# Peer experts of the first half: dots before sums, sums shared two to one between TensorE and VectorE, projected tiles copied by ScalarE, keys loaded earlier

## The chip, the core and the metric

The kernel runs on one core of a Trainium2 chip. The metric is the device time of one execution in microseconds (us). PE is TensorE, DVE is VectorE, ACT is ScalarE, POOL is GpSimd, SP is SyncE.

## What is computed

Two blocks of a network over 512 tokens of width 1024, all in float32. The change touches the first block, above all its layer of "peer" experts:

```python
q = (xb @ w_query).reshape(T, 8, 2, 128)                  # 8 heads, two halves of a query
s = einsum('thpk,hpnk->thpn', q, sub_keys)                # scores against 128 keys
top_s, top_i = top_k(s, 16)                               # 16 best of each, 256 pairs, 16 best pairs
best_s, best_pos = top_k(cand_s, 16); idx = ...; gate = softmax(best_s)
u = expert_u[idx]; v = expert_v[idx]                      # a row of 1024 floats for each pick
act = gelu(einsum('td,thkd->thk', xb, u))                 # "dots"
y = einsum('thk,thkd->td', gate * act, v)                 # "sums"
```

Each token has 8 x 16 = 128 picks. For each pick and each tile of 128 tokens one row of the table u and one of the table v are gathered (128 partitions x 4 KB, 524,288 bytes). Ahead of the peer layer stands a mixer (a projection to 3584 columns, a gated linear recurrence named hgrn, a short convolution, an output projection), behind it the second block.

## The kernel before

The tokens are split into half A (tiles 0 and 1) and half B (tiles 2 and 3). Half A runs first through the first mixer, its query projection and the picks of tile 0. Then a long block opens (`Stretch`) in which half B's mixer, query projection and picks run as the main work, and the peer layer of half A runs beside them on DVE, POOL and PE. Stages inside it end with `meet`, where SP, PE, ACT and DVE wait for each other; POOL does not take part.

**The side work.** `Peer.sequence` writes a fixed plan of steps: one step is one gathered row, either a dot (table u) or a sum (table v). POOL gathers the rows in the order of the plan into a ring of 12 slots (L1496); slot n is refilled once step n-12 has been consumed. A dot is one fused multiply-and-accumulate on DVE (L1574). A sum of tile 1 is one fused multiply-add on DVE (L1580), and each waits for the one before. A sum of tile 0 goes by PE: DVE makes a diagonal matrix of the coefficients (L1568, eight buffers), and PE multiplies the gathered row with it, adding up in banks 0 and 1 (L1593, four matmul records for a row). A sum needs the Gelu of its tile's dots, which ACT does at the first `meet` after the tile's last dot has been put in the program (L1508).

In the plan before, the 128 dots of tile 0 come first, then 98 dots of tile 1 (`FRONT` = 226), then 32 groups of four PE sums of tile 0 and one further dot of tile 1 (30 dots are left), then the 128 DVE sums of tile 1.

**Who places the steps.** The code of the main work calls `beside(m, dve, us)` at many places. `Peer.go` adds that time to a credit and places steps while the credit is at least `pace`: in the front a dot costs 1.1 of credit, later a DVE step costs 1.8 and a PE sum 0.75. PE sums are allowed from `reach_front` on, which `key_scores` calls once half B's scores of its first tile are copied; `reach_front` first places what is missing up to `FRONT`. What the credit did not place by the end of half B's picks is placed in `Peer.finish`, a stage of its own with nothing else in it but a prefetch of 4 MB of weights, which waits for the last PE sum.

**Half B's stages, in order**, with their names in the prediction:
- first projection: 12 tiles of 128 columns (L345 on PE, 16 matmul records for a tile; `project`). DVE copies each tile out of its bank (L1046). In `setup`, ahead of the first copy, DVE finishes the picks of tile 0 (`pick_rest`): its last part waits for an exponential on ACT (L1313, issued by `exp_next`, which is passed as `other`). Between the tiles DVE does the 14 parts of tile 1's picks.
- second projection: 16 tiles, copied by DVE (L1049), with the short convolution in `setup`
- hgrn in three stages, and a group norm
- output projection: 8 tiles, kept by a multiply-add on DVE (`add_projected`, L1060)
- norm; SP issues the loads of the keys into `keys_raw` (L1112)
- turn back: PE transposes h into rows (L1085) and then the keys (L1125), ACT copies the latter (L1132)
- query projection: 16 tiles, copied by DVE (L1706)
- scores and picks (`key_scores`): PE multiplies queries and keys (L1232), DVE copies tile 0's scores (L1249), ACT tile 1's (L1240); DVE picks, 14 parts for each of two tiles, with 5.0 us of credit behind each part
- finish: the rest of the plan; then PE's sums are copied out of the banks (L1603)

After that the norms and the second block's mixer of half A follow, with half B's peer steps beside them.

## Time and profile before

| | us |
|---|---|
| median of 3 runs | 3729.78 (3722.16 to 3733.29) |
| profiled execution, its own time | 3702.43 |
| span of its profile | 3700.6 |

Over the whole span the page gives PE 74% busy, DVE 58%, POOL 35%, ACT 16%, and 272 GB/s moved by DMA; 40 equal slices of the span show DVE at 7 to 9 tenths from the fifth slice to the twenty-third. The change touches the stretch from 372 to 1298 us of the span. A timeline row reads: start, duration, engine, line, operation, output <- input, count, and in brackets the idle time before it with what ended it. Durations of DVE overlap slightly: the start-to-start time of two neighbours is what an instruction costs its engine.

### The profile page before, as it was taken

What the parts mean: (1) busy time and instruction counts of PE and PEld (TensorE: products, weight loads), DVE (VectorE), ACT (ScalarE), POOL (GpSimd) and SP (SyncE); (2) the same over time, 40 slices, a digit from 0 to 9 for tenths busy, and PEclk for the clock granted to TensorE, in tenths of its full rate; (3) what the DMA queues carried; (4) which work ended last, traced back from release to release, by engine and by line L of the source; (5) the groups of instructions that cost most, each with busy time, mean ns of one, the idle gap of its engine ahead of it and who ended that gap; (6) DMA issues with size and microseconds to landing.
All of it is one profiled execution on the core that took longest, in us unless ns stands there. A gap on an engine that the chain in (4) does not pass through costs nothing. (4 is left out here: it accounts for less than half of the span.)

```text
span 3700.6 us, 44636 instructions
## 1 busy us (share of the span) xinstructions
PE 2746.5 (74%) x17746; PEld 1979.5 (53%) x17746; DVE 2136.4 (58%) x3975; ACT 592.3 (16%) x1229; POOL 1311.7 (35%) x1082
## 2 busy tenths in 40 slices
PE   5977553678880086889885757799999789777777
PEld 4866443464330075677773636478888667322232
DVE  6544999878748977968777988424222453200001
ACT  1021002200000012122212310132222330100001
POOL 0001366666767765757655566300000000000000
PEclk7988776788995587889987778999999889899998
DMA  7616588888999988889979699622333324899997
GB/s 273 229 40 222 198 293 317 299 326 328 329 343 370 376 310 302 312 309 369 356 259 362 219 336 363 227 91 87 101 101 96 117 80 172 331 428 428 428 429 321
DMA packets 390749, 1006.30 MB, mean 272 GB/s; under 512 B 30381, under 2 KB 234515, under 8 KB 375699
## 3 DMA queue, kind: packets, MB, share of 16 engines
q0 software_dynamic: 150912, 549.52, 40.0%
q1 hardware_dynamic: 211856, 406.65, 29.9%
q10 hardware_dynamic: 27779, 47.38, 3.5%
q8 instruction: 134, 2.20, 0.2%
q14 instruction: 68, 0.56, 0.0%
HBM read 971.99 MB, written 31.46 MB: 271 GB/s over the span
## 5 line engine op out<-in xcount | busy, mean ns | idle before, releaser
L1496 POOL DMA_INDIRECT ring<-in_peer_u_dram,index x512 | 685.0, 1338 | 448.0 <-DVE ring L1574 240.4
L1496 POOL DMA_INDIRECT ring<-in_peer_v_dram,index x512 | 597.4, 1167 | 334.6 <-DVE h_rows_b L1580 144.6
L345 PE MATMUL bank<-hT,weights 128*128 128x256 f32 x1984 | 459.3, 396 | 144.5 <-ACTq L142 72.3
L345 PEld LDWEIGHTS bank<-hT,weights 128*128 128x128 f32 x1984 | 394.6, 200 | 208.6 <-issue 130.0
L1891 PE MATMUL bank<-hT,weights 128*128 128x256 f32 x1792 | 431.2, 396 | 6.5 <-DVE weights L2089 4.1
L1891 PEld LDWEIGHTS bank<-hT,weights 128*128 128x128 f32 x1792 | 343.2, 196 | 60.9 <-DVE weights L2089 4.5
L1574 DVE SCALAR_TENSOR_TENSOR ring<-ring,h_rows_a 128x1024 f32<-128x1024 f32 x256 | 305.1, 1223 | 60.4 <-DMA ring<-in_peer_u_dram,index 56.4
L1580 DVE SCALAR_TENSOR_TENSOR h_rows_b<-ring,coef,h_rows_b 128x1024 f32<-128x1024 f32 x238 | 305.2, 1283 | 43.3 <-DMA ring<-in_peer_v_dram,index 23.2
L1574 DVE SCALAR_TENSOR_TENSOR ring<-ring,h_rows_b 128x1024 f32<-128x1024 f32 x256 | 299.4, 1223 | 4.4 <-DMA ring<-in_peer_u_dram,index 4.0
L2908 POOL IOTA mo_down<- 128x4 f32 x1 | 0.1, 144 | 792.5 <-POOLq L160 792.5
L1593 PE MATMUL bank<-ring,weights 128*128 128x512 f32 x512 | 227.4, 606 | 20.6 <-DVE weights L1568 13.7
L3210 DVE COPY weights<-bank 128x512 f32<-128x512 f32 x16 | 11.1, 691 | 296.1 <-PE bank L3146 296.1
L1593 PEld LDWEIGHTS bank<-ring,weights 128*128 128x128 f32 x512 | 99.2, 195 | 148.3 <-issue 147.1
L1580 DVE SCALAR_TENSOR_TENSOR h_rows_a<-ring,coef,h_rows_a 128x1024 f32<-128x1024 f32 x127 | 163.1, 1284 | 14.0 <-DVE h_rows_a L1580 0.9
L2227 DVE TENSOR_TENSOR rc_Y<-rc_Y,bank 128x512 f32<-128x512 f32 x40 | 27.4, 684 | 231.3 <-PE bank L2194 216.3
L3107 POOL DMA_INDIRECT weights<-h_kept,mo_columns x16 | 15.0, 938 | 395.9 <-PE bank L3120 378.3
L3134 PE MATMUL bank<-xp_near,weights 128*64 128x512 f32 x512 | 127.7, 658 | 36.4 <-DMA xp_near<-in_w_exp_gate_dram 25.1
L3134 PE MATMUL bank<-xp_far,weights 128*64 128x512 f32 x512 | 126.2, 650 | 36.3 <-DMA xp_far<-in_w_exp_gate_dram 23.7
L1736 PE MATMUL bank<-ident,h_rows_a 128*128 128x128 f32 x16 | 3.7, 425 | 190.8 <-issue 190.8
L345 PE MATMUL bank<-ssd_y,weights 128*128 128x256 f32 x512 | 118.7, 397 | 12.1 <-ACTq L142 9.4
L345 PEld LDWEIGHTS bank<-ssd_y,weights 128*128 128x128 f32 x512 | 101.8, 200 | 29.6 <-issue 14.2
L1736 PEld LDWEIGHTS bank<-ident,h_rows_a 128*128 128x128 f32 x16 | 3.3, 228 | 191.6 <-issue 191.6
(570 smaller groups left out, 4290.8 us busy)
## 6 DMA issues: line engine op xcount, KB each, us to landing
weights<-in_w_in_dram SPq DMA_DIRECT2D x112, 512.0 KB, 3.8
weights<-in_w_in_dram SPq DMA_DIRECT2D x54, 1024.0 KB
xp_near<-in_w_exp_gate_dram SPq DMA_DIRECT2D x9, 4096.0 KB, 34.3
xp_far<-in_w_exp_up_dram SPq DMA_DIRECT2D x9, 4096.0 KB, 33.2
xp_near<-in_w_exp_up_dram SPq DMA_DIRECT2D x7, 4096.0 KB, 33.9
xp_far<-in_w_exp_gate_dram SPq DMA_DIRECT2D x7, 4096.0 KB, 35.7
xp_near<-in_w_exp_down_dram SPq DMA_DIRECT2D x7, 4096.0 KB, 34.4
xp_far<-in_w_exp_down_dram SPq DMA_DIRECT2D x7, 4096.0 KB, 34.4
```

Of the source, the lines that this page charges most:

```text
L345: ins = pe.matmul(m.ps[b][:, 0:TH], m.weights[:, s, k, c * P:(c + 1) * P], rhs(k), start=(k == 0), stop=(k == k_tiles - 1))
L1496: pool.indirect_dma_start(out=self.ring[:, n % RING, :], out_offset=None, in_=self.tables[table], in_offset=bass.IndirectOffsetOnAxis(ap=s ...
L1574: dve.scalar_tensor_tensor(out=slot, in0=slot, scalar=1.0, in1=row, op0=ALU.mult, op1=ALU.mult, accum_out=dots[:, j:j + 1]).then_inc(self. ...
L1580: dve.scalar_tensor_tensor(out=row, in0=slot, scalar=coef[:, j:j + 1], in1=row, op0=ALU.mult, op1=ALU.add).then_inc(self.free, 1)
L1593: ins = pe.matmul(bank[:, :], diag[:, j % self.DIAGS, :], self.ring[:, n % RING, h * 512:(h + 1) * 512], start=(j in (0, PICKS)), stop=(j ...
L1736: ins = pe.transpose(m.ps[k][:, t * P:(t + 1) * P], rows[:, t, k * P:(k + 1) * P], m.ident[:, :])
L1891: ins = pe.matmul(self.m.ps[3 + pair % 2][:, c * TH:(c + 1) * TH], self.weights[:, (i + 2) % self.SLOTS, k % (KT // 2), c * P:(c + 1) * P] ...
L2227: dve.tensor_tensor(dst[:, :, :], dst[:, :, :], bank3(5 + j), ALU.add).then_inc(xy_kept, 1)
L2908: iota = lambda ap, pat, b, cm: c.link(pool, pool.iota(ap, pat, base=b, channel_multiplier=cm, allow_small_or_imprecise_dtypes=True))
L3107: pool.indirect_dma_start(out=self.xr[:, p % 2, :], out_offset=None, in_=self.h_rows, in_offset=bass.IndirectOffsetOnAxis(ap=columns[:, p: ...
L3134: ins = pe.matmul(m.ps[2 + j][q, :], self.xT[:, k, q], self.ring[slots[j]][:, h, k * DE:(k + 1) * DE], start=(k == 0), stop=(k == KT - 1))
L3210: dve.tensor_copy(self.hidT[:, :, :].rearrange("p k r -> p (k r)"), self.m.ps[4][:, :]).then_inc(self.h_kept, 1)
```

## The change

It does five things.
1. The plan: all 256 dots of half A first (`FRONT` = 256), then 64 groups of two PE sums of tile 0 and one DVE sum of tile 1, then the other 64 DVE sums.
2. `key_scores`: after `reach_front`, ACT's Gelu of tile 1 (`m.side.activate`) is placed behind ACT's score copies and ahead of its exponentials.
3. `project` gets `copied`: ACT copies each tile out of its bank, and DVE no longer waits for the tile. Used in half B for the first and second projection and for the query projection.
4. Half B's keys are loaded by ACT in the output projection, into half A's `h`, which is free by then, and not by SP in the norm.
5. The keys are loaded by eight DMAs and not four, in both halves.

```diff
@@ project
+        if copied:
+            @block.scalar
+            def _(act):
+                for t in range(n_tiles):
+                    act.wait_ge(m.tile_made, made0 + t + 1)
+                    act.copy(copied(t), m.ps[t % per_turn][:, 0:TH]).then_inc(m.tile_kept, 1)
+
         if other:
             other(block, made0, kept0)
...
             for t in range(n_tiles):
-                dve.wait_ge(m.tile_made, made0 + t + 1)
-                keep(dve, t, m.ps[t % per_turn]).then_inc(m.tile_kept, 1)
+                if not copied:
+                    dve.wait_ge(m.tile_made, made0 + t + 1)
+                    keep(dve, t, m.ps[t % per_turn]).then_inc(m.tile_kept, 1)
                 if hook:
                     hook(dve, t)
                 beside(m, dve, 0.44 * k_tiles)
@@ first_mixer, both projections
-                setup=setup, hook=hook, other=other)
+                setup=setup, hook=hook, other=other,
+                copied=None if half.first else lambda t: proj[:, t + 16, :])
@@ first_mixer, output projection
-        add_projected(m, half, w_out[0], mixed, KT, m.mod[:, 2 * KT:3 * KT], then)
+        add_projected(m, half, w_out[0], mixed, KT, m.mod[:, 2 * KT:3 * KT], then, other4)
@@ Keys
+    def lay_over(self, rows):
+        self.raw = rows
+
+    def load_by(self, eng):
+        for k in range(KT):
+            eng.dma_start(self.raw[:, k, :].rearrange("p (j n) -> p j n", n=P),
+                          self.src[:, 2 * k:2 * k + 2, :]).then_inc(self.landed, 16)
...
+    def load_beside(self, block, made0, kept0):
+        @block.scalar
+        def _(act):
+            self.load_by(act)
@@ key_scores: the same instructions, ACT's placed behind reach_front, and
+            m.side.activate(act)
             picker.exp(act, i0)
             picker.exp(act, i0 + 1)
@@ Peer
-    FRONT = 226
-    GROUP = 4
+    FRONT = 2 * PICKS
+    GROUP = 2
...
-        second_dots, first_sums = all_of(1, 0), all_of(0, 1)
-        steps, at = all_of(0, 0), self.FRONT - PICKS
-        steps += second_dots[0:at]
-        for j in range(0, PICKS, self.GROUP):
-            steps += first_sums[j:j + self.GROUP] + second_dots[at:at + 1]
-            at += 1
-        steps += second_dots[at:] + all_of(1, 1)
+        pe_sums, dve_sums = all_of(0, 1), all_of(1, 1)
+        steps = all_of(0, 0) + all_of(1, 0)
+        for j in range(PICKS // self.GROUP):
+            steps += pe_sums[j * self.GROUP:(j + 1) * self.GROUP] + dve_sums[j:j + 1]
+        steps += dve_sums[PICKS // self.GROUP:]
@@ first_experts
-            norm(m, half.x, half.h, m.scale2, m.mod[:, 3 * KT:4 * KT], other=keys.load)
+            norm(m, half.x, half.h, m.scale2, m.mod[:, 3 * KT:4 * KT], other=keys.load if half.first else None)
...
         project(m, w_query[0], 2 * PH, lambda k: half.h[:, k, :], KT,
-                lambda dve, t, bank: dve.tensor_copy(qT[:, t, :], bank[:, 0:TH]))
+                None, copied=lambda t: qT[:, t, :])
@@ two_blocks
+                        keys = Keys(m, peer_sub_keys[0])
+                        keys.lay_over(first.h)
                         first_mixer(m, second, columns, w_in, w_out, levels.masks, carry, work, (peer_w_query[0], 2 * PH),
-                                    setup=pick_rest, hook=pick_next, other=exp_next)
+                                    setup=pick_rest, hook=pick_next, other=exp_next, other4=keys.load_beside)
```

## Rows read from the trace of the kernel before

**Rows 1.** First line of the page: the span.
```profile
span 3700.6 us, 44636 instructions
```
**Rows 2.** Busy time by stage: length, busy us (instructions), PEclk, DMA share, GB/s.
```profile
core 0: us, PE busy (x) PEld busy (x) DVE busy (x) ACT busy (x) POOL busy (x), PEclk, DMA share, GB/s
377.00:496.00 119.00, 42.46 (x183) 36.01 (x182) 117.81 (x356) 0.56 (x2) 51.04 (x37) 0.70 0.62 208
496.00:586.00 90.00, 60.11 (x256) 51.30 (x256) 78.46 (x148) 0.00 (x0) 69.68 (x51) 0.84 0.99 365
...
742.00:763.00 21.00, 7.35 (x32) 6.55 (x32) 6.16 (x12) 2.29 (x4) 9.84 (x9) 0.50 0.83 316
763.00:840.00 77.00, 60.27 (x256) 51.49 (x256) 65.20 (x117) 0.05 (x1) 55.76 (x44) 0.90 0.89 335
...
863.00:1085.00 222.00, 204.91 (x464) 89.50 (x464) 161.58 (x593) 0.62 (x2) 157.18 (x145) 0.96 0.92 337
1085.00:1298.00 213.00, 22.46 (x48) 9.70 (x48) 169.04 (x145) 1.59 (x2) 151.81 (x140) 0.56 0.98 364
...
1360.00:1500.00 140.00, 95.00 (x350) 72.12 (x348) 110.57 (x183) 30.86 (x77) 91.41 (x66) 0.79 0.85 306
```
**Rows 3.** Timeline of PE and ACT in half B's first projection.
```profile
372.76 7.61 PE L345 MATMUL bank<-hT,weights 128*128 128x256 f32 x21 [17.46 <-PEq L160]
379.78 30.60 PE L345 MATMUL bank<-hT,weights 128*128 128x256 f32 x141
386.55 0.26 ACT L1313 ACTIVATE pk_ex<-pk_ex 128x64 f32<-128x64 f32 x1 [29.09 <-DVE pk_ex L1404]
```
**Rows 4.** Timeline of DVE there: end of tile 0's picks, a copy, two dots.
```profile
394.37 0.21 DVE L1425 TENSOR_REDUCE pk_total<-pk_ex 128x4 f32<-128x64 f32 x1
...
396.23 0.42 DVE L1046 COPY proj<-bank 128x256 f32<-128x256 f32 x1
396.58 0.29 DVE L1332 MAX8 pk_val<-work 128x8 f32<-128x128 f32 x1
...
400.82 1.22 DVE L1574 SCALAR_TENSOR_TENSOR ring<-ring,h_rows_a 128x1024 f32<-128x1024 f32 x1
...
401.96 1.22 DVE L1574 SCALAR_TENSOR_TENSOR ring<-ring,h_rows_a 128x1024 f32<-128x1024 f32 x1
```
**Rows 5.** Waits from 377 to 1300 us: total, times, longest.
```profile
ACT hT L391 <- DVEq L149: 39.4, 1, 39.4
...
DVE coef L1561 <- ACTq L142: 23.8, 1, 23.8
...
DVE qT L1706 <- PE bank L345: 19.6, 1, 19.6
...
PEld bank L1125 <- DMA keys_raw<-in_peer_sub_keys_dram: 12.9, 1, 12.9
```
**Rows 6.** Groups of instructions from 863 to 1085 us (scores and picks).
```profile
L1593 PE MATMUL bank<-ring,weights 128*128 128x512 f32 x464 | 204.9, 604 | 13.9 <-DVE weights L1568 13.7
...
L1574 DVE SCALAR_TENSOR_TENSOR ring<-ring,h_rows_a 128x1024 f32<-128x1024 f32 x29 | 35.6, 1229 | 39.8 <-DMA ring<-in_peer_u_dram,index 37.8 <-issue 1.7
L1568 DVE TENSOR_SCALAR weights<-ident,coef 128x128 f32<-128x128 f32 x118 | 27.8, 297 | 13.6 <-remote 9.3 <-issue 1.7 <-PE bank L1593 1.7
```
**Rows 7.** Timeline: scores loaded, first diagonals, two gathers, PE's last sums.
```profile
858.39 1.23 DVE L1318 COPY work<-weights 128x2048 f32<-128x2048 f32 x1
...
863.18 0.88 DVE L1568 TENSOR_SCALAR weights<-ident,coef 128x128 f32<-128x128 f32 x4
...
1081.54 0.94 POOL L1496 DMA_INDIRECT ring<-in_peer_v_dram,index  x1 [0.30 <-issue]
1082.78 0.94 POOL L1496 DMA_INDIRECT ring<-in_peer_v_dram,index  x1 [0.30 <-issue]
...
1085.21 22.46 PE L1593 MATMUL bank<-ring,weights 128*128 128x512 f32 x48 [6.76 <-remote]
```
**Rows 8.** Timeline of DVE in the finish: first coefficients, sums, PE's sums copied out.
```profile
1118.02 0.29 DVE L1561 TENSOR_TENSOR coef<-coef,gate 128x128 f32<-128x128 f32 x1 [23.75 <-ACTq L142]
...
1198.77 23.50 DVE L1580 SCALAR_TENSOR_TENSOR h_rows_a<-ring,coef,h_rows_a 128x1024 f32<-128x1024 f32 x17
...
1296.85 1.29 DVE L1603 COPY h_rows_a<-bank 128x512 f32<-128x512 f32 x2 [0.60 <-DVE h_rows_a L1580]
```
**Rows 9.** Groups of instructions from 377 to 1298 us: the tile copies.
```profile
L1706 DVE COPY qT<-bank 128x256 f32<-128x256 f32 x16 | 6.8, 422 | 19.6 <-PE bank L345 19.6
L1049 DVE COPY proj<-bank 128x256 f32<-128x256 f32 x16 | 6.7, 417 | 0.0
L1046 DVE COPY proj<-bank 128x256 f32<-128x256 f32 x12 | 5.0, 420 | 0.0
```

54 lines of the change are left out of this document (30 added, 24 removed).

## The prediction

> **What bounds the kernel now.** The change lives in the stretch from 372 to 1298 us of a span of 3700.6 us [rows 1], so I read the busy times by stage first, and there the DVE column against the stage's length. In the first projection DVE is busy 117.8 of 119.0 us [rows 2]: it is the bound, since tile 1's picks and the dots fill it. The second projection moves 365 GB/s with a DMA share of 0.99. From 763 to 840 PE is busy 60.3 of 77 us, and DVE waits 19.6 us for PE's tiles in order to copy them [rows 2, 5]. From 742 to 763 almost nothing computes: DVE is busy 6.2 of 21 us, and PE waits 12.9 us for the keys [rows 2, 5].
>
> Then come the two big stages. In scores and picks (863 to 1085) PE is busy 204.9 of 222 us with 464 records, which is 116 sums at 204.9/116 = 1.77 us [rows 2, 6]. PE is the bound, while DVE stands idle some 60 us. The finish (1085 to 1298) is the opposite: PE works the first 22.5 us [rows 7], DVE then stands 23.8 us until the Gelu of tile 1 is there [rows 5, 8], and from there DVE alone adds rows, 17 in 23.50 us, 1.38 us each [rows 8]. So PE's sums and DVE's sums stand one behind the other, each bound by its own engine: 227 us on PE (128 x 1.77) and 177 us on DVE (128 x 1.38). That is what the new plan overlaps.
>
> **Part 1, the tile copies.** A copy costs DVE 396.58 - 396.23 = 0.35 us from start to start [rows 4]. ACT is idle there (0.6 of 119 us busy [rows 2]), so the copies cost nothing on their own; without that cover they would cost about the 0.42 us each that DVE's take [rows 9].
> - First projection: 12 x 0.35 = 4.2 us less on its bound. But the copies come ahead of `exp_next` in ACT's program, and ACT works in order. Today ACT makes tile 0's late exponential at 386.6 [rows 3], and DVE reads it at 394.4 [rows 4], without a wait. Afterwards ACT first has to copy 12 tiles, and the twelfth is there only when PE has made 12 x 16 = 192 records. PE had made 21 + 141 = 162 by 379.78 + 30.60 = 410.4 [rows 3]; 30 more at 30.60/141 = 0.217 us give 416.9, the copy and the exponential 417.6. DVE stands from 394.4 to 417.6, 23.2 us, and everything of DVE is queued behind it: tile 1's picks and the dots. POOL has filled its 12 slots and stands too. Net here: +23.2 - 4.2 = **+19.0 us**. Bounds: +15 if PE runs without a break at its best pace, +25 if it waits for weights.
> - Second projection: 16 x 0.35 = 5.6 us less DVE work, in a stage that moves 365 GB/s. Bounds 0 and -5.6; I take **-3**.
> - Query projection: DVE no longer waits for tiles. It has 51 dots at 401.96 - 400.82 = 1.14 us, 58 us, and PE 60.3 us plus its waits for weights of some 8 us, against 77 now [rows 2, 4]. PE becomes the bound at 68 to 74 us; DVE's faster start makes gathers compete with the weights, so I take **-6** (bounds -9 and -2).
>
> **Part 2, the keys.** They are loaded 40 us earlier on ACT, whose next work (the squares of the norm) comes after an idle time of 39.4 us [rows 5]; eight issues fit in that from every side. SP loses four issues in half B and gains four in half A, where the norm covers them. PE's 12.9 us [rows 5] go: **-12**. DVE is late next, with its copies and dots.
>
> By these the scores of half B, loaded at 858.4 [rows 7], would be there at 858.4 + 19.0 - 3 - 6 - 12 = 856.4.
>
> **Part 3, `reach_front`.** Adding up the credits of `beside` up to there gives 248.9 us, at 1.1 for a dot 226 dots: today `reach_front` finds its 226 already placed and does nothing. Afterwards it places 30 more, ahead of the picks: 30 x 1.14 = **+34 us**, in which PE has nothing to do. The ring holds 12 of these rows, and the other 18 come at 1.24 us each (two gathers' start to start [rows 7]), so DVE sets the pace. These 30 dots leave the picks, where they stand now.
>
> **Part 4, the picks.** 28 parts with 5.0 us of credit are 140 us. A group of two PE sums and a DVE sum takes 2 x 0.75 + 1.8 = 3.3, so 42 groups are placed: 85 PE sums and 42 DVE sums. (Today's 4 x 0.75 + 1.8 = 4.8 gives 29 groups, and the rows show 29 dots and 118 diagonals [rows 6].) DVE is busy 161.6 us from 863 to 1085; less 29 dots (33.1) and 118 diagonals at 0.88/4 = 0.22 (26.0) that leaves 102.5 us of picks [rows 2, 6, 7]. Afterwards:
> - DVE: 4.8 (858.4 to 863.2) + 102.5 + 85 x 0.22 + 42 x 1.38 = 184
> - PE: 85 x 1.77 = 150
> - POOL: 127 gathers at 1.24 to 1.39 (the sums' pace in the finish) = 157 to 177
>
> DVE is the bound, with the gathers close. Now the bounding engine loses 13.9 us of 222 to others [rows 6]; three near each other lose no less. I add 10: **194 us**, bounds 184 and 215. The stage then runs from 856.4 + 34 = 890.4 to 1084.4, which is where it ends today.
>
> **Part 5, the finish.** It has 43 PE sums and 86 DVE sums, and no wait for the Gelu, which ACT now does during the picks. First 21.5 groups: PE 43 x 1.77 = 76 us, gathers 64 x 1.3 less the 12 in the ring = 68; then 64 DVE sums x 1.38 = 88. The 4 MB of weights that today load while DVE stands idle now load beside these sums; at 374 GB/s, which that stretch can move, they cost 11 us if nothing hides them, 0 if the ring does; I take 5. Two for the start and one for the copy at the end: 76 + 88 + 5 + 3 = **172 us**, against 213 now [rows 2]. Bounds 165 and 190. End: 1084.4 + 172 = 1256 against 1298.
>
> The sum is -42 us; the terms of the front are the least certain and lean to the slow side, so I take **-40**. The profiled execution took 3702.4 us; this gives 3662. It is 27 us below the median of the runs, 3729.8, and I carry the difference over: 3690. What follows 1298 us is untouched and only shifts.
>
> **A rule against the change.** The rows show how much the core can move: 365 GB/s with other loads beside the gathers, 364 in the finish [rows 2], and 524,288 bytes each 1.24 us where POOL is free [rows 7], 423 GB/s. The Trainium skill, "DMA: Bandwidth & Descriptors", section "Where 436 GB/s comes from", puts the limit of HBM for one core at about 358 GB/s. By that rule a gather takes 1.46 us and rival B below is the forecast, with some 27 us of gain; the trace disagrees as far as single stretches go, and no row shows a long one above 375.
>
> **Rivals.**
> - A, the forecast: 3690, own range 3668 to 3706. 0.56.
> - A+, everything overlaps and the front loses less: -65 us, 3665. DVE's idle time, 60 + 44 us from 863 to 1298 [rows 2], leaves room. 0.08.
> - B, the gathers become the bound: from the scores on, 512 - (226 + 12) = 274 rows and 8 rows' worth of weights are to be moved. At 370 GB/s (1.42 us) that is 400 us, from 856 to 1256, plus 20 us that the picks leave unused: -22, 3708. For it: shares of 0.92 and 0.98 in both stages [rows 2]. Against: DVE's sums already ran at 1.38 us when their rows had long been in the ring. 0.17.
> - C, the ring ties the engines together: its slots come free in plan order, so a slow PE sum holds up the next DVE sum. If they alternate without overlap, a group costs 2 x 1.77 + 1.38 = 4.9 us, the picks 42 x 4.9 = 207 and the finish 21.5 x 4.9 + 88 + 8 = 201: 890 + 207 + 201 = 1298, no gain, 3730. For it: POOL waits for PE now, and dots wait 37.8 us for rows [rows 6]. Against: in the picks DVE has 2.4 us of other work for each group that PE can use. 0.11.
> - D, slower: PE's clock. PE sums run at 0.96 of full clock while PE is busy 92% [rows 2]. With pauses the granted clock falls: 0.90 at 78% busy (763 to 840), 0.79 at 68% (1360 to 1500) [rows 2]. Mine is 77% in the picks. At 1.2 GHz a sum takes 3.5 us, all 128 take 453 from 895, and the last 64 DVE sums follow: the end is at 1425, +127, 3857. It decides from 2.57 us for a sum on, (1298 - 895 - 88 + 14)/128, a mean clock of 0.69. The Trainium skill, "TensorE: Matmul & The Clock Gate", section "Why this matters for your kernels", also warns that idle gaps between bursts bring the lower clock. The rows say 0.8 to 0.9, which costs nothing here, since PE has 40 us to spare in the picks. 0.08.
>
> **How the numbers follow.** About 0.3%, 11 us, is what a measurement of this kernel can tell from no change. A, A+ and four fifths of B lie beyond it on the fast side: 0.56 + 0.08 + 0.14 = 0.78 faster. C and the rest of B are the same: 0.14. D is 0.08 slower. The range of 8 in 10 reaches from 3660, inside A+, to 3724, which takes in B and the half of C that falls short of no gain.
>
> **What would show it.** Right: ACT's first exponential of the stretch near 417 and DVE idle just before it for 23 us; no wait of PE on the keys; 30 dots in a row near 856 to 890; L1580 rows between the parts of the picks; no wait of L1561 on ACT at the start of the finish; the finish near 172 us. Wrong: L1593 records well above 0.6 us with PEclk below 0.7; DVE waiting for rows of the v table in the picks by more than 30 us; a first projection that ends no later than 496; a second half, from the norms on, that is longer by itself.

## The result: 0.7% slower, where 1% faster was forecast

The changed kernel took 3743.48 us (median of 12 runs, 3731.43 to 3756.77) beside 3715.75 for the kernel before in the same comparison (12 runs, 3705.70 to 3733.29): a ratio of 1.007, interval 1.0052 to 1.0087. A second comparison on another chip (e9 below) gave 1.0054, 1.0033 to 1.0076. Ratios are of executions in the fast state alone, which leaves out one of e17 below (4349.18 us) and the profiled one of e1 (3744.61 us). The profiled execution of the changed kernel took 3739.1 us, its span 3737.2, against 3700.6 before: 36.6 more, of which 6.7 are there by the norms behind the first half's finish (1298.5 before, 1305.2 now). By the medians it is 27.7 more.

The busy times by stage of the changed kernel, for [rows 2]: first projection, start of the second, what is left between keys and query projection, query projection, the dots of `reach_front`, the picks, and the finish in two parts, up to PE's last sum and behind it:

```profile
core 0: us, PE busy (x) PEld busy (x) DVE busy (x) ACT busy (x) POOL busy (x), PEclk, DMA share, GB/s
377.00:515.00 138.00, 39.41 (x182) 34.35 (x181) 113.04 (x344) 4.93 (x14) 51.93 (x37) 0.65 0.55 179
515.00:605.00 90.00, 58.52 (x256) 50.32 (x256) 71.73 (x129) 5.98 (x16) 70.10 (x50) 0.82 0.99 364
765.00:773.00 8.00, 6.35 (x34) 6.09 (x35) 6.28 (x11) 2.15 (x4) 6.48 (x6) 0.69 0.87 302
773.00:848.00 75.00, 58.05 (x256) 50.00 (x254) 61.61 (x102) 5.96 (x16) 60.37 (x49) 0.89 1.02 385
867.00:909.00 42.00, 2.12 (x11) 1.87 (x9) 35.46 (x59) 2.46 (x3) 33.79 (x23) 0.54 0.76 246
909.00:1106.00 197.00, 156.52 (x323) 65.47 (x324) 171.89 (x561) 2.21 (x4) 156.88 (x124) 0.89 0.92 330
1106.00:1203.00 97.00, 86.29 (x190) 33.90 (x188) 38.84 (x70) 0.00 (x0) 72.76 (x69) 1.00 0.98 372
1203.00:1305.00 102.00, 0.21 (x1) 0.00 (x0) 83.51 (x67) 0.00 (x0) 80.92 (x67) 0.52 1.01 382
```

The first row is 138 us long for 119 before, because tile 0's exponential now comes behind the 12 copies. The stage of the keys is 8 us for 21. The fifth row is new: 42 us with 2.1 us of PE. The picks take 197 us (194 were forecast) with DVE busy 172 of them, so the bounding engine is the one that was named. The finish takes 97 + 102 = 199 us, 14 less than before and 27 more than forecast: first PE is busy 86 of 97 us, then DVE 84 of 102, and behind either stand a DMA share of 0.98 to 1.01 and 372 to 382 GB/s.

ACT and DVE in the first projection of the changed kernel (timelines; before: [rows 3, 4]):

```profile
start us, us, engine line op out<-in xcount [idle before <-releaser]
378.24 0.37 ACT L361 COPY proj<-bank 128x256 f32<-128x256 f32 x1 [21.78 <-PE bank L346]
...
416.23 0.37 ACT L361 COPY proj<-bank 128x256 f32<-128x256 f32 x1 [3.08 <-PE bank L346]
416.50 0.26 ACT L1343 ACTIVATE pk_ex<-pk_ex 128x64 f32<-128x64 f32 x1
```
```profile
416.79 0.22 DVE L1455 TENSOR_REDUCE pk_total<-pk_ex 128x4 f32<-128x64 f32 x1 [23.42 <-ACT pk_ex L1343]
```

The waits of the changed kernel from 377 to 1305 us (before: [rows 5]), those that matter:

```profile
engine line waited for: us in total, times, longest us
...
DVE h_rows_a L1608 <- DMA ring<-in_peer_v_dram,index: 84.5, 55, 4.8
PE bank L1621 <- DVE weights L1596: 74.0, 18, 45.2
...
DVE pk_total L1455 <- ACT pk_ex L1343: 23.4, 1, 23.4
```

The 23.8 us for the Gelu are gone, as is PE's wait for the keys. In their place stand 84.5 us in which DVE waits for rows of the v table, in 55 pieces, and one of 45.2 in which PE waits for its first diagonal. The groups of the changed kernel from its first sum on PE to the norms (914 to 1305 us; the last number before `|` is the mean in ns; for [rows 6]):

```profile
L1524 POOL DMA_INDIRECT ring<-in_peer_v_dram,index x249 | 300.0, 1205 | 82.7 <-issue 75.9 <-PE bank L1621 4.7 <-remote 2.1
L1621 PE MATMUL bank<-ring,weights 128*128 128x512 f32 x512 | 243.0, 629 | 91.1 <-DVE weights L1596 74.0 <-issue 12.6 <-DMA ring<-in_peer_v_dram,index 2.5
L1608 DVE SCALAR_TENSOR_TENSOR h_rows_a<-ring,coef,h_rows_a 128x1024 f32<-128x1024 f32 x127 | 163.5, 1288 | 93.6 <-DMA ring<-in_peer_v_dram,index 84.5 <-issue 4.3 <-DVE h_rows_a L1608 0.8
```

POOL fills the stretch: 300 us busy, and 75.9 of its 82.7 idle us are the 0.30 us that stand before each gather. It waits 4.7 us for slots of the ring. So it starts a row every 1.53 us, where the forecast gave it 1.24 to 1.39. Stage by stage, its gathers and the 0.30 us before each take 193 of the 197 us of the picks, 91 of the 97 and all of the 102. The same view of the kernel before, over its own stretch (863 to 1298 us):

```profile
L1496 POOL DMA_INDIRECT ring<-in_peer_v_dram,index x246 | 261.9, 1065 | 120.0 <-issue 64.8 <-PE bank L1593 43.8 <-DVE h_rows_a L1577 10.5
```

There a gather of the same rows takes 1.07 us instead of 1.21, and POOL had 54 us of waits for slots to spare. In the finish alone, before (1085 to 1298 us) and in the changed kernel's last part (1203 to 1305):

```profile
L1496 POOL DMA_INDIRECT ring<-in_peer_v_dram,index x129 | 140.0, 1085 | 59.1 <-issue 35.7 <-PE bank L1593 12.1 <-DVE h_rows_a L1577 10.5
```
```profile
L1524 POOL DMA_INDIRECT ring<-in_peer_v_dram,index x60 | 73.6, 1226 | 20.7 <-issue 20.7
```

That made me suspect POOL and the rows' bytes first; the experiments had to say how much of the 84.5 us they are.

### The profile page after: what moved, and what is told of

It reads as the page before. It is cut to its first block and busy times, and to the rows that moved or that the text cites. A ratio compares the mean times of both kernels' runs of the same rounds, so it can differ in the third digit from the quotient of the medians.

```text
span 3737.2 us, 44633 instructions
## 1 busy us (share of the span) xinstructions
PE 2771.1 (74%) x17746; PEld 1988.2 (53%) x17746; DVE 2117.4 (57%) x3931; ACT 609.4 (16%) x1273; POOL 1362.5 (36%) x1082
## 5 line engine op out<-in xcount | busy, mean ns | idle before, releaser
L1524 POOL DMA_INDIRECT ring<-in_peer_u_dram,index x512 | 701.7, 1370 | 450.8 <-DVE ring L1602 242.3
L1524 POOL DMA_INDIRECT ring<-in_peer_v_dram,index x512 | 632.3, 1235 | 317.1 <-DVE h_rows_b L1608 167.1
L1621 PE MATMUL bank<-ring,weights 128*128 128x512 f32 x512 | 243.0, 629 | 91.1 <-DVE weights L1596 74.0
L1608 DVE SCALAR_TENSOR_TENSOR h_rows_a<-ring,coef,h_rows_a 128x1024 f32<-128x1024 f32 x127 | 163.5, 1288 | 93.6 <-DMA ring<-in_peer_v_dram,index 84.5
L3163 PEld LDWEIGHTS bank<-xp_far,weights 128*64 128x64 f32 x512 | 40.7, 152 | 120.2 <-issue 95.3
```

The costliest lines, as they stand in the source:

```text
L1524: pool.indirect_dma_start(out=self.ring[:, n % RING, :], out_offset=None, in_=self.tables[table], in_offset=bass.IndirectOffsetOnAxis(ap=s ...
L1608: dve.scalar_tensor_tensor(out=row, in0=slot, scalar=coef[:, j:j + 1], in1=row, op0=ALU.mult, op1=ALU.add).then_inc(self.free, 1)
L1621: ins = pe.matmul(bank[:, :], diag[:, j % self.DIAGS, :], self.ring[:, n % RING, h * 512:(h + 1) * 512], start=(j in (0, PICKS)), stop=(j ...
L3163: ins = pe.matmul(m.ps[2 + j][q, :], self.xT[:, k, q], self.ring[slots[j]][:, h, k * DE:(k + 1) * DE], start=(k == 0), stop=(k == KT - 1))
```

## Experiments

The comparisons ran on five chips, and these differ: the kernel before has medians of 3709.9 to 3716.7 us on three of them, 3622.0 and 3622.8 on two. Ratios are each with the kernel before on the same chip; stretches are compared within one group of chips. Four markers serve throughout: the scores' first record on PE, the first sum on PE, the norms of the first half, the norms of the second (all from the PE timeline).

**First group: the change taken apart (chip of 3709.9 us).** e1 sets the leftover credit behind the finish back; e2 puts the late exponential ahead of the copies; e3 is the kernel before with the new plan alone; e4 the changed kernel with the old plan.

```diff
 e1, in finish
-        self.pace = LATE_PACE
+        self.pace, self.time = LATE_PACE, 1.14
 e2, in project, ahead of ACT's copies (called with exp_late, taken out of exp_next)
+                if first_of_all:
+                    first_of_all(act)
 e4, in Peer (and the loop of sequence as before)
-    FRONT = 2 * PICKS
-    GROUP = 2
+    FRONT = 226
+    GROUP = 4
```

> The changed kernel, but the credit that is left when half A's plan is done is set to 1.14, what it is in the kernel before (the changed one has 1.74 there). From the norms on, the program is then the kernel before's, step for step. Theory P (placement): the 30 us that the stretch from half A's norms (1305 us) to half B's norms (2403 us) took more than before come from this one number, which moves every DVE step of half B's rows by up to one place. Then that stretch falls from 1098 to 1068 us and the time lies 30 us below the changed kernel's, near 3713. Rival S (scatter): the stretch varies from run to run by itself, by how the transfers fall. Then it has no tie to the credit, and the time stays within 10 us of 3743.

> The changed kernel, but ACT makes tile 0's late exponential ahead of the 12 tile copies. Its input is there at 386 us, so the copies start 8 us later than now at most, and PE has 8 banks to fill meanwhile. Theory (the exponential behind the copies): DVE's wait of 23.4 us in the first projection goes, that projection ends near 492 and not 514.8, and the time falls by 20 to 24 us to some 3721. Rival (the gathers are the bound of the whole stretch): the same number of rows has to come in less time, so half of it comes back as waits for rows further on, and the time falls by 12 us or less.

> The kernel before with the new plan alone: FRONT 256, groups of two PE sums and one DVE sum, the Gelu of tile 1 in the picks. No copies on ACT, keys loaded in the norm. Theory B (gathers are the bound from the scores on, in the old plan as in the new): the stretch from the loading of the first scores (858 us) to half A's norms (1298 us) stays 440 us within 8 us, and the time is within 12 us of before, apart from what the leftover credit does further on. Theory A (the forecast, engines were the bound): the stretch falls to 400 us, the time by 40 us.

> The changed kernel with the old plan (FRONT 226, groups of four and one). Copies on ACT, the exponential behind them, and the early keys stay. Theory: the first projection still costs 19 us more and the keys give 13 back, the query projection up to 6; half A's norms start at 1298 plus or minus 6, and the leftover credit is the old one, 1.14, so that the stretch up to half B's norms is 1068 us again and the time is within 10 us of before. If instead the new plan is what costs, this kernel lies well below the changed one in the stretch from 858 to the norms, by 15 us or more.

| | ratio (interval) | scores | first sum | norms A | norms A to B |
|---|---|---|---|---|---|
| before (first profile) | 1 | 840.5 | 863.6 | 1298.5 | 1067.9 |
| changed (first profile) | 1.007 (1.0052 to 1.0087) | 848.3 | 914.3 | 1305.2 | 1097.7 |
| e1 | 0.9993 (0.9965 to 1.002) | 852.1 | 915.0 | 1309.7 | 1098.1 |
| e2 | 0.9961 (0.9941 to 0.9982) | 824.0 | 888.4 | 1280.4 | 1084.3 |
| e3 | 1.0013 (0.9986 to 1.004) | 839.2 | 897.5 | 1283.3 | 1088.5 |
| e4 | 0.9992 (0.997 to 1.0014) | 844.8 | 866.3 | 1296.0 | 1093.3 |

ACT in e2's first projection, the exponential first:

```profile
385.45 0.26 ACT L1345 ACTIVATE pk_ex<-pk_ex 128x64 f32<-128x64 f32 x1 [29.05 <-DVE pk_ex L1436]
385.61 0.90 ACT L363 COPY proj<-bank 128x256 f32<-128x256 f32 x3
```

The order of one activation is worth 24.8 us at the norms (1305.2 to 1280.4; 29.3 from e1, the changed kernel's program up to there on this chip) and takes the kernel from slower to faster than before. The ratio fell by more than that, from 1.007 on the one chip to 0.9961 on the other; some 13 us of it lie behind the norms (1084.3 for 1097.7), and no run says why. The new plan alone has its norms 15.2 us earlier than before, not 40, and its time is the same as before: from the scores to the norms 444.1 us for 457.9, which is neither theory's. e4's norms are 2.5 us early: with the old plan the late scores cost almost nothing, because its picks and finish absorb them. The parts don't add: -15.2 (e3) and -2.5 (e4) make +6.7 together, since the old plan makes good most of the 23 us: from e4 to e14, the same line moved under the old plan and on another of the slower chips, the norms come only 7.6 us earlier. That this slack is the 54 us in which POOL waits for slots there was not tested. Behind the norms e4 was to have 1068 us again and has 1093.3. e1's median has no loss, but its profiled execution (3744.6 us) lies at the top of its runs and shows the changed kernel's own 1098.1, so e12 repeats it.

**Second group: are the bytes the bound? (chip of 3622.0 us.)** e5 and e6 gather half rows for the first half, in the kernel before and the changed one (by the edit an index counts half rows of the table, so as many pieces of half the length come, but not the first halves of the rows picked); e7 is e2 with the old plan; e8 the kernel before, unchanged.

```diff
+            wide = D // 2 if n < self.HALF_STEPS else D
-                out=self.ring[:, n % RING, :], out_offset=None, in_=self.tables[table],
+                out=self.ring[:, n % RING, 0:wide], out_offset=None,
+                in_=self.tables[table] if wide == D else self.tables[table].rearrange("e (h d) -> (e h) d", h=2),
```

> The kernel before, in which each of the first half's 512 gathers brings only the first half of a row (2 KB per partition instead of 4 KB, from the same number of rows); the arithmetic keeps its full width on what the slot holds, and the dots scale by 0.1. It leaves out half of every gathered row of that half. Together with its twin on the changed kernel it asks what bounds the stretch from the first sum on TensorE to the norms behind the finish: 434.9 us in the kernel before, 390.9 in the changed one (and 458.0 against 456.9 from the scores on). Theory B (the bytes of the gathers bound both plans, 348 and 345 GB/s over the whole stretch): the old plan has its engines as a bound nearly as tight, PE 116 x 1.77 = 205 and some 10 of waits, then 22 + 24 of PE and the Gelu and some 110 sums of DVE at 1.29 = 142, together about 403, so here 395 to 420 from the first sum on, 15 to 40 less than before. Theory C (the ring ties the engines): the same for this kernel, 400 to 425. The twin tells them apart.

> The changed kernel with the same half-wide gathers for the first half's 512 rows (half of each gathered row is left out). Theory B (bytes): DVE's 84.5 us of waits for rows of the v table shrink to under 20, and the engines' own work is left: about 184 us of picks and 76 + 64 x 1.29 + 5 = 164 of finish at most, so 335 to 355 us from the first sum on TensorE to the norms, against 390.9. Theory C (ring order, slots come free in plan order, PE and DVE hand over to each other): the alternation stays whatever the width, 380 to 395, with DVE's waits for rows nearly as long as before since POOL still cannot start a gather before a slot is free. A third way, that POOL's own work for a gather sets the pace (1.2 us each whatever it brings): 256 gathers from the first sum at about 1.2 us would be 307 us or less, which would leave the stretch near 350 as in B, but with POOL busy over 90 per cent and waits for rows still over 40 us.

> The changed kernel with the old plan (226 steps in front, four sums on PE to one step on DVE) and with the late exponential ahead of ACT's tile copies: it keeps the copies on ACT and the early keys alone. Theory B with the queue on ACT as the second cost: the changed kernel with the old plan gave 0.9992 of the time before with the exponential's 23 us still in it; without them some 20 to 25 us less, a ratio of 0.992 to 0.995, 3683 to 3692 us beside a 3710 of the kernel before. Rival (all that starts earlier is eaten by the same bytes, since the gathers from 763 us on are bound by the memory): the scores come 20 us earlier, but the norms behind the finish do not: a ratio of 0.997 to 1.0. If the new plan has a gain of its own of over 10 us that needs the early start, then the run of the changed kernel with the exponential first (0.9961) is the faster one.

> The kernel before, unchanged, for a second profile and for the scatter. The stretch from the norms behind the first half's finish to the norms of the second took 1067.9 us in its first profile and 1084 to 1098 in five profiles of other kernels whose program there is the same but for one step. Theory S (it is the scatter of one execution): this profile gives another value, between 1075 and 1100, and the ratio is 1.0 within 0.002. Theory T (the change costs some 20 to 30 us there in a way not yet found): it gives 1068 within 5 us again.

First sum to norms: 418.3 us in e8 and 420.1 in e5 (825.5 to 1245.5); and 380.7 in e6, where the unchanged plan has 379.9 and 371.3 on the other fast chip (e9, e12 below). Half the bytes did nothing for this stretch in either plan. What they gave the kernel before came ahead of it: its scores are there at 811.4 us for 842.7. e6's picks and the two parts of its finish:

```profile
898.00:1086.00 188.00, 154.61 (x328) 65.21 (x328) 171.02 (x559) 2.21 (x4) 150.55 (x124) 0.92 0.61 172
1086.00:1188.00 102.00, 83.86 (x186) 33.24 (x184) 38.37 (x72) 0.00 (x0) 80.98 (x70) 1.00 0.63 176
1188.00:1284.00 96.00, 0.39 (x2) 0.04 (x1) 84.43 (x68) 0.00 (x0) 75.10 (x69) 0.52 0.79 241
```

The DMA share falls to 0.61 and 172 GB/s, and only the last part is a little shorter. DVE still waits for rows:

```profile
DVE h_rows_a L1609 <- DMA ring<-in_peer_v_dram,index: 81.6, 33, 3.9
```

POOL is busy 296.0 us there and has 69.8 of the 0.30 us pieces, 366 of 381: it is as full as in the changed kernel, whatever a gather brings. That is the third way of the expectation in its mechanism, though not in its 350 us; C's 380 to 395 us fit the time, so the next group and e13 had to tell them apart. (e5 and e6 took 3587.7 and 3634.4 us in one run each, where the kernel before has 3622.0.) e7 gave 0.9955 (0.9931 to 0.9978), just above the 0.992 to 0.995 that were expected; e8 1.0003 (0.9988 to 1.0019), and with 1009.1 us between the norms it fits neither of its theories, since this chip differs from the first by more than both allowed.

**Third group: POOL beside VectorE (chip of 3622.8 us).** In the trace of the changed kernel POOL's gathers are 0.94 us in some rows and up to 4.38 in others, with the same work. POOL from 1040 to 1047 us in the changed kernel, and what DVE did under the long one:

```profile
1040.10 0.94 POOL L1524 DMA_INDIRECT ring<-in_peer_v_dram,index  x1 [0.30 <-issue]
1041.34 1.08 POOL L1524 DMA_INDIRECT ring<-in_peer_v_dram,index  x1 [0.30 <-issue]
1042.72 4.38 POOL L1524 DMA_INDIRECT ring<-in_peer_v_dram,index  x1 [0.30 <-issue]
```
```profile
1043.97 2.31 DVE L1413 TENSOR_TENSOR work<-pk_val 128x2048 f32<-128x2048 f32 x1
1046.32 1.28 DVE L1608 SCALAR_TENSOR_TENSOR h_rows_a<-ring,coef,h_rows_a 128x1024 f32<-128x1024 f32 x1
```

Setting each of the 255 gathers from 914 to 1305 beside what DVE did most of its time gives means of 0.96 us beside an idle DVE (55), 1.28 beside DVE's sums (100) and 2.0 to 4.3 beside the picks' operations on 2048 columns with two SBUF operands (13: L1380, L1384, L1413). Beside L1386, a reduction that is as long (2.29 us) and reads one operand, it is 0.94 (4). The Trainium skill, "SBUF — State Buffer", section "SBUF: two separate sides", says that GpSimd and a VectorE operation in a 2-port mode or with two SBUF inputs arbitrate for one port pair, as an exclusive lock, and its box on SWDGE that behind a 2-port operation GpSimd can't write a DMA's descriptors; these rows agree in kind, and e10 tests it. e9 is the changed kernel again, e10 has DVE's sums of the first half in PSUM, e11 that and the exponential first, e12 the credit.

```diff
+        elif tile == 1:
+            if j:
+                dve.wait_ge(self.free, self.rank[n])
+            for h in range(D // 512):
+                part, bank = slot[:, h * 512:(h + 1) * 512], m.ps[2 + h][:, :]
...
+                    ins = dve.scalar_tensor_tensor(out=bank, in0=part, scalar=coef[:, j:j + 1], in1=bank,
+                                                   op0=ALU.mult, op1=ALU.add)
+            ins.then_inc(self.free, 1)
```

> The changed kernel, unchanged, beside the kernel before and the next three on one chip. What it is for: the loss behind the first half's norms. In the first two profiles the stretch from those norms to the second half's norms took 1067.9 us before and 1097.7 after; a second profile of the kernel before had 1009.1 there, with 1190 records of TensorE in 100 us of the projections where the first had 980 to 1090. Theory S (it is how fast the memory gives the weights in an execution, no part of the change): here 0 to 10 us more than a kernel of the old plan in the same call, and a ratio near 1.002 to 1.004, what the 7 us up to the norms make. Theory T (the change costs 20 to 30 us there): 1.007 again. Up to the norms both say +5 to +12.

> The changed kernel with one thing altered: the first half's sums on VectorE accumulate in two PSUM banks (two instructions of 512 columns for a row) instead of an SBUF row, and are copied out at the end. Nothing is left out. POOL's gather instruction takes 0.94 us at the least, 1.00 beside an idle VectorE and 1.29 on average beside one of those sums, which read two operands from SBUF (96 gathers from 914 to 1305 us); a gather starts every 1.53 us. Theory P (POOL, writing the gathers' descriptors, sets the pace and VectorE's sums with two SBUF operands hold it up): the mean of a gather there falls from 1.20 to 1.05 to 1.10 us, and the stretch from the first sum on TensorE to the norms by 15 to 35 us, to 356 to 376 on the chip of the first profile; the ratio 0.995 to 1.001. Theory M (the memory's bytes alone set the pace): the gathers' mean and the stretch stay, 385 to 393, and the ratio is that of the unchanged kernel. Theory V (a sum into PSUM costs VectorE more than 1.28 us): the stretch grows if a pair takes over 1.5 us.

> The same sums in PSUM, with the late exponential ahead of ACT's tile copies besides: a candidate that may beat both kernels. The exponential alone took the changed kernel from 1.007 to 0.9961. Theory P: 15 to 35 us on top of that where POOL's pace is freed, a ratio of 0.987 to 0.993. Theory M: 0.995 to 0.998, as with the exponential alone.

> The changed kernel with the credit that is left over at the end of the first half's finish set to the 1.14 us of the kernel before, so that the program behind it places its dots exactly as before. In its first run the ratio was 0.9993 against 1.007 for the changed kernel in another call, while its profile showed no gain. If the placing matters, it is 15 to 25 us faster than the unchanged kernel in this call; if it was the scatter of calls, the two agree within 7 us.

| | ratio (interval) | first sum | norms A | between | norms A to B |
|---|---|---|---|---|---|
| e7 (old plan) | 0.9955 (0.9931 to 0.9978) | 838.6 | 1256.6 | 418.0 | 1011.1 |
| e8 (old plan) | 1.0003 (0.9988 to 1.0019) | 855.2 | 1273.5 | 418.3 | 1009.1 |
| e9 | 1.0054 (1.0033 to 1.0076) | 905.7 | 1285.5 | 379.9 | 1022.5 |
| e10 | 1.0068 (1.0043 to 1.0093) | 898.8 | 1271.8 | 373.0 | 1018.0 |
| e11 | 0.9987 (0.9967 to 1.0007) | 878.6 | 1252.7 | 374.0 | 1025.1 |
| e12 | 1.0022 (1.0 to 1.0044) | 900.5 | 1271.8 | 371.3 | 1025.0 |

POOL and DVE's sums from the first sum to the norms in e12 (whose program is the changed kernel's up to there; POOL's row), and in e10:

```profile
L1524 POOL DMA_INDIRECT ring<-in_peer_v_dram,index x248 | 284.1, 1145 | 76.3 <-issue 70.7 <-PE bank L1621 5.6
```
```profile
L1524 POOL DMA_INDIRECT ring<-in_peer_v_dram,index x247 | 247.1, 1001 | 105.6 <-issue 50.0 <-DVE bank L1612 30.8 <-PE bank L1632 24.9
L1612 DVE SCALAR_TENSOR_TENSOR bank<-ring,coef,bank 128x512 f32<-128x512 f32 x254 | 179.4, 751 | 62.1 <-DMA ring<-in_peer_v_dram,index 57.4 <-DVE bank L1612 0.5
```

The mechanism is there: without the second SBUF operand a gather beside a sum takes 0.94 us (129 gathers), and POOL's busy time falls by 37 us. The gain isn't: 373.0 us lies between the two profiles of the unchanged plan. POOL now waits 56 us for slots. In e12, picks and the two parts of the finish take 186, 92 and 99 us; in e10 they take 183, 90 and 105, the last because a row costs DVE 1.50 us (2 x 0.751) instead of 1.28, which is theory V. The two effects can be told apart only roughly. Three rows bound what is to be had from faster rows (e12, the same three stages):

```profile
895.00:1081.00 186.00, 150.38 (x318) 63.25 (x319) 172.05 (x563) 2.21 (x4) 147.76 (x124) 0.91 0.95 349
1081.00:1173.00 92.00, 87.03 (x195) 35.46 (x194) 38.90 (x70) 0.00 (x0) 70.34 (x72) 1.00 1.01 402
1173.00:1272.00 99.00, 0.16 (x1) 0.17 (x2) 83.10 (x68) 0.00 (x0) 78.89 (x67) 0.52 1.02 392
```

DVE is busy 172 of 186, PE 87 of 92, DVE 83 of 99. Each stage has an engine that fills it but for 5 to 16 us, 35 in all; in e9 these losses are 42, in the changed kernel's first profile 25, 11 and 18, together 54. In e10 they are 24 (7, 5 and 12), while DVE's own work in picks and last part has grown by 14. So the slow gathers cost this plan 11 to 18 us, which the dearer sums took back; a run that frees POOL without making DVE's sums dearer is missing. DVE's 84.5 us of waits for rows are mostly slack of an engine that was not the bound there (it is busy 39 us of the 97 in which PE sums).

e11 did not beat e7, and its 0.9987 is worse than either theory had it. e9 has 13.4 us more between the norms than e8, and a ratio of 1.0054, between what its two theories gave. e12's median is 8 us below e9's, its interval overlaps e9's, and its norms A to B are as long: in the profiles the credit is not the cause of the loss behind the norms, though the medians leave room for a few us.

**Fourth and fifth group: what else could hold it (chips of 3716.7 and 3715.9 us).** e13 joins e6 and e10. e14 is e7 again. e15 has a third plan: 226 dots in front, then groups of two sums on PE and one step of DVE, the 30 dots first; e16 that with PSUM sums. e17 and e18 use 10 of the ring's 12 slots, in the changed kernel and the one before.

```diff
 e15, in sequence
+        own, late = all_of(1, 1), second_dots[at:]
+        for j in range(0, PICKS, self.GROUP):
+            steps += first_sums[j:j + self.GROUP] + [late.pop(0) if late else own.pop(0)]
+        steps += own
 e17, e18
-RING = 12
+RING = 10
```

> The changed kernel with half-wide gathers for the first half's 512 rows (half of each gathered row is left out) and with VectorE's sums of that half in PSUM. Half-wide alone left the stretch from the first sum to the norms at 380.7 us, PSUM alone took it from 379.9 to 373.0. Theory L (two limits lie close behind each other, the memory's bytes and POOL's descriptor writing beside VectorE; taking one away shows the other): both away give POOL 256 gathers at 1.25 to 1.35 us, 320 to 345 us, and VectorE its own work, 64 x 1.50 + about 200, near 340; I expect 335 to 355. Theory C (the order of the ring holds the engines together whatever each costs): 365 or more.

> The changed kernel with the old plan and the late exponential first (0.9955 before), beside the next two on one chip: 0.994 to 0.998 again.

> A third plan on that kernel: 226 dots in front as before, so TensorE starts its sums with the scores; then groups of two sums on TensorE and one step of VectorE, which is one of the 30 dots left until they are done and a sum of VectorE from then on; tile 1's Gelu stands between ACT's two exponentials of the picks. Nothing is left out. If the 30 dots with TensorE idle (some 50 us from the scores to its first sum) are a true cost of the new plan, and VectorE standing 41 us for rows and 23 us for the Gelu one of the old, this one avoids both: first sum to norms 385 to 405 us against 407 with the old plan, and a ratio of 0.990 to 0.994. If the gathers' pace is all that counts (about 290 rows at 1.40 us or more from the scores to the norms, whatever the plan), the norms come where they come with the old plan, within 5 us, and the ratio is within 0.0015 of the kernel with the old plan.

> The third plan with VectorE's sums of the first half in PSUM besides. POOL's gathers beside these sums take 0.94 us instead of 1.25 to 1.29, but a row's sum takes VectorE 1.50 us instead of 1.28. If POOL's pace decides, 5 to 12 us less than the third plan alone; if VectorE is the bound by now (116 or so sums x 0.22 us more), up to 20 us more.

> The changed kernel with a ring of 10 slots instead of 12 (all of its gathers, nothing left out). Half-wide gathers, sums in PSUM and both together left the stretch from the first sum to the norms at 380.7, 373.0 and 406.6 us, against 371 to 395 in four profiles of the plan itself. A row was summed 8.0 us after its gather's instruction had ended where VectorE waited for it (26 of the last 58 rows), so ten slots at 1.5 us, 15 us, would still cover that. Theory C (the ring's order holds the three engines together: a slot is given back only when the slower of two engines has taken its row, and the 12 slots are all the slack there is): a sixth of the slack less costs 12 to 40 us in this stretch, to 395 to 430, and POOL's waits for PE's slots grow from under 12 us to over 25. Theory L (bytes or POOL's pace): under 5 us more, and POOL waits for no slot.

> The kernel before with 10 slots. In its plan TensorE and VectorE take turns of long stretches and do not hand over row by row, and POOL already waits 48 us for slots of PE. Theory C says that it is less sensitive than the changed plan: first sum to norms 0 to 15 us more than 418 to 435. If it loses as much as the changed plan or more, the slack of the ring is no mark of the new plan.

| | ratio (interval) | first sum | norms A | between | norms A to B |
|---|---|---|---|---|---|
| e13 | one run, 3749.4 us | 905.7 | 1312.3 | 406.6 | 1104.9 |
| e14 | 0.9998 (0.9979 to 1.0016) | 850.3 | 1288.4 | 438.2 | 1096.8 |
| e15 | 0.9988 (0.9962 to 1.0014) | 850.3 | 1275.0 | 424.6 | 1099.3 |
| e16 | 0.9991 (0.997 to 1.0012) | 850.0 | 1287.0 | 437.0 | 1097.3 |
| e17 | 1.0076 (1.0039 to 1.0112) | 907.4 | 1297.5 | 390.1 | 1097.2 |
| e18 | 1.0037 (1.0004 to 1.0071) | 864.0 | 1300.2 | 436.2 | 1102.9 |

e13 is the clearest miss: 406.6 us for an expected 335 to 355. Its waits from 914 to 1300:

```profile
DVE bank L1613 <- DMA ring<-in_peer_v_dram,index: 54.0, 24, 5.0
POOL ring L1525 <- PE bank L1633: 44.9, 25, 6.8
POOL ring L1525 <- DVE bank L1613: 24.2, 31, 4.5
PE bank L1633 <- DVE weights L1597: 23.4, 8, 9.4
PE bank L1633 <- remote: 18.5, 4, 6.2
DVE pk_ind L1366 <- issue: 10.5, 15, 1.3
DVE weights L1597 <- issue: 9.6, 4, 8.2
...
DVE bank L1613 <- remote: 3.9, 1, 3.9
```

My 335 to 355 had forgotten that PE's part of the finish stands between the two of DVE. By e13's own stages DVE is busy 180 of 208 us in the picks, PE 86 of 93, DVE 94 of 111 in the tail (1.50 us a row). So rows that come with half the bytes and beside no conflict leave the engines' own work and 52 us more, 28 of them in the picks. Of these 28 DVE waited 5.4 us for rows; for 21.5 the profile names neither an engine nor a transfer ("issue" is time in which an engine waited for nothing that the profile shows, and behind "remote" stands no instruction of this core), where e10's picks have none of that. So e13 is no proof of rival C's mechanism, though its 406.6 us are over C's 365, and what holds it is open; some 11 to 20 us of its distance to e10's 373.0 are what the slower chips take more for this stretch of the unchanged plan (390.9 for 379.9 and 371.3). A smaller ring does not bring C's price either: with 10 slots (e17) the stretch stays at 390.1 for 390.9, and POOL's waits for PE's slots are 18.7 us, not over 25; e18's stretch did not move either (436.2 for 434.9). Where e18's 1.0037 comes from is open. e15 has its norms 13.4 us before e14's, so the third plan gains up to there, but 424.6 us miss the expected 385 to 405, and 0.9988 can't be told from no change. (Its expectation compares with 407 us for the old plan, which is e7's 418.0.) It has no 42 us of dots without PE, and pays for it with 30 more of DVE's steps behind PE's last sum (144 us for 102). PSUM sums cost this plan the gain again (e16), because DVE is its bound. e14's 0.9998 against e7's 0.9955 of the same program: the gain of the early keys and copies seems to depend on the chip; it was run on one of each kind.

## Why the prediction was wrong, by its own steps

1. **First projection**: DVE waited 23.42 us (forecast 23.2), and the stage's end moved from 496.3 to 514.8, +18.5 (+19.0). Right, and e2 shows it by taking it away.
2. **Second and query projections**: -3 and -6 were forecast, +4.1 and -1.4 came (from the first projection's end to the output projection 188.2 to 192.3 us, of which the second projection is a part; the query projection 77.1 to 75.7). The copies moved from DVE freed next to nothing in stages where the DMA moves 364 and 385 GB/s at shares of 0.99 and 1.02. Together 12 us too good.
3. **Keys**: -13.5 for -12. Right.
4. **`reach_front`**: 30 dots as forecast, 867.0 to 909.0, 42 us for 34: nine waits for rows, 6.4 us in all. With 10.6 us from points 1 to 3 (867.0 for 856.4), the picks begin 19 us late.
5. **Picks**: 197 us for 194, DVE the bound (busy 172), with POOL as full. Right in time. POOL's gathers were costed too low, 1.24 to 1.39 us for what is 1.53 from start to start over picks and finish: 1.24 came from two rows with no sum of DVE beside them, 1.39 from the old finish, where a gather took 1.08 us beside sums that ran back to back. e10 shows that the second SBUF operand makes gathers slow; its price over picks and finish is the 11 to 18 us above.
6. **Finish, the step that failed**: 199 us for 172, outside its bounds of 165 to 190. "First 21.5 groups: PE 43 x 1.77 = 76 us": it was 97. PE had 128 - 323/4 = 47 sums left, not 43, because it starts 5 us behind DVE in the picks and its sums wait there for diagonals; at 86.29/(190/4) = 1.82 us each these are 86 us; and in 11 us more PE waits, above all for diagonals and rows, in a part that POOL fills but for 6 us. "Then 64 DVE sums x 1.38 = 88", with 8 for the weights and ends: it was 102, in which POOL had no pause (60 gathers of 1.23 us for this half, each with 0.30 before it, and 7 for the next), so that DVE waited 14.0 us for rows. The forecast counted 1.3 us for a gather in the first part and let none set the pace in the second. It was not the bytes, or hardly: with half of them (e6) the two parts take 102 and 96 us, where the plan itself takes 92 and 99, or 92 and 101, on the same kind of chip (e12, e9).
7. **"What follows is untouched and only shifts."** On the three slower chips the stretch from norms to norms is 1084 to 1105 us for either plan; the 1067.9 of the first profile of the kernel before is alone, and the forecast took that execution, 13 us under the median of its comparison, for its base. On one of the faster chips the old plan has 1009.1 to 1011.1 there (e8, e7, e5) and the new one 1018.5 (e6), on the other the new plan has 1018.0 to 1025.1 (e9 to e12): some 8 us or more that the forecast had at nothing. Their cause is open; the profiles say that the credit (e12) is not it.

The sum in the trace: from -42 at the norms, +11 (points 1 to 3), +8 (dots), +3 (picks), +27 (finish) make +7, and +6.7 was measured. Behind the norms stand the other 29.8: 9 of them are the choice of the two profiled executions (36.6 us between them, 27.7 between the medians), some 8 are point 7, and the rest is open. Up to the norms the terms of an overlap were each taken at the best row, and the own work of the three engines in turn (DVE 35 + 172, PE 86, DVE 84 = 377 of 438 us from the scores' end to the norms) left only 61 us for everything between them. Of the rivals, C's 442 us (34 + 207 + 201) was nearest to what came (42 + 197 + 199 = 438), B had 420, the forecast 400. C's number is a coincidence: its PE and DVE take turns, but in the picks they were busy 157 and 172 of 197 us. B was nearer in kind: the gathers do pace the last part, but by POOL's instructions and not by their bytes. D did not come: PE's granted clock in the picks was 0.89. The rule that was weighed, the Trainium skill's 358 GB/s of HBM ("DMA: Bandwidth & Descriptors", "Where 436 GB/s comes from"), is exceeded here: 402 GB/s held for 92 us (e12, above) and 393 for 200 us (e8, below). The gain of 27 us that the forecast gave for that rule left out the 20 us that rival B adds; with them its own numbers make about 9.

## What to carry to other kernels

Before work is moved onto an idle engine, list what already stands in that engine's program behind the place where it goes: 12 copies of 0.37 us cost 23 us, because one activation of 0.26 us was queued behind the last of them, and moving that one line ahead is worth more here (24.8 us at the norms) than the new plan (15.2). When a plan is to overlap two engines, add up for each stage what its fullest engine has to do, with the means of rows in which both work; do so for the engine that issues their gathers too (255 rows at 1.53 us are all of the 391 us here); and count what the plan adds without overlap (42 us of dots with PE idle, as much as the overlap won). And take the base of a sum from more than one profiled execution where a stretch bounded by memory follows.

## What was not expected of the hardware

- **Chips differ by 2.5% in the same program.** For the first profile of the kernel before and e8, the same program, spans are 3700.6 and 3617.3: 25 us apart up to the norms, 59 between the norms, nothing behind (1334.3 and 1334.8 us). The two rows are of 200 us in the second half's projections, 300 us behind the first half's norms, in the one and the other:

```profile
1598.00:1798.00 200.00, 182.35 (x2145) 153.88 (x2145) 155.24 (x269) 48.16 (x92) 127.80 (x96) 0.91 0.89 323
```
```profile
1573.00:1773.00 200.00, 190.58 (x2380) 163.58 (x2380) 182.03 (x309) 53.38 (x105) 154.68 (x116) 0.97 1.03 393
```

323 against 393 GB/s, 2145 against 2380 records of PE. The same program gained on one chip (e7, 0.9955) and not on another (e14, 0.9998).
- **A gather's instruction on POOL takes 0.94 us by itself, 1.28 on average beside the changed kernel's VectorE sums, which read two SBUF operands of 1024 columns, and up to 4.38 beside operations on 2048.** With half the bytes per row it is 1.26 beside the sums (e6). Beside the sums of the kernel before it is 1.10 (125 gathers); why less is open. With one operand and the result in PSUM it stays at 0.94 (e10), and VectorE pays 0.75 us for 512 columns there.
- **Ten slots serve as well as twelve** in the first half: a row that DVE waited for was summed 8.0 us after its gather's instruction had ended (26 rows in the last 100 us of the changed kernel; 9.8 us in e12), and ten slots at 1.5 us cover that. The stretch from the first sum to the norms took 390.1 us with ten (e17) and 390.9 with twelve.
